# The opening of a two-block transformer kernel: c as a small tile, four modulation tiles on TensorE, another order of the first products

## What is computed

```python
c_act = silu(c)                              # c: 1 x 1024
mod = c_act @ ada_w[0] + ada_b[0]            # 6 x 1024; shift_t, scale_t are its first two parts
h = rmsnorm(x, norm_g[0, 0]) * (1.0 + scale_t) + shift_t
q, k, v, r, a_lr = split(h @ w_in)           # gated linear attention follows
```

## Time and profile before

| | us |
|---|---|
| three runs | 1540.8, 1542.72, 1542.75 |
| median | 1542.72 |
| the profiled execution | 1540.82 |
| its span | 1539.5 |
| TensorE, VectorE, ScalarE busy | 1513.5, 985.3, 660.6 |
| mean granted TensorE clock | 0.999 of 2.4 GHz |

### The profile page before, as it was taken

The page is one execution under the profiler, slowest core; times in us unless marked ns, Lnnn a source line. Parts: engine busy times, 40 slices in busy tenths (PEclk is TensorE's granted clock), DMA queues, the critical chain, the costliest instruction groups (busy, mean ns, idle before and its releaser), DMA issues.

```text
span 1539.5 us, 18851 instructions
## 1 busy us (share of the span) xinstructions
PE 1513.5 (98%) x7498; PEld 1235.9 (80%) x7498; DVE 985.3 (64%) x1592; ACT 660.6 (43%) x1118; POOL 163.9 (11%) x153
## 2 busy tenths in 40 slices
PE   8999999999999999999999999999999999999998
PEld 6778878888888888777777878888888876888776
DVE  7567667866666664777776743434344539989764
ACT  6445434513233233455565532413233436555660
POOL 0000002000000002111111100000000102675200
PEclk9999999999999999999999999999999999999999
DMA  9344444566656553122212243333333222212131
GB/s 370 120 129 148 140 137 161 167 215 192 194 189 200 185 162 98 55 69 69 69 56 83 96 117 96 96 96 96 98 94 102 72 87 68 70 53 75 37 109 55
DMA packets 52458, 181.82 MB, mean 118 GB/s; under 512 B 5793, under 2 KB 6689, under 8 KB 52370
## 3 DMA queue, kind: packets, MB, share of 16 engines
q1 hardware_dynamic: 52370, 180.61, 37.4%
HBM read 177.05 MB, written 3.41 MB: 117 GB/s over the span
## 4 chain that ended last, share of the span: by engine, by line
PE 90%; DVE 4%; ACT 2%; POOL 2%; DMA 1%; issue 1%; SPq 0%; DVEq 0%; ACTq 0%
PE PS L520 24%; PE PS L523 23%; PE PS L521 23%; PE PS L530 2%; PE PS L531 2%; PE PS L533 2%; PE PS L576 2%; PE PS L912 1%; PE PS L757 1%; PE PS L776 1%; PE PS L595 1%; PE PS L1067 1%; POOL sb_TMD L2345 1%; PE PS L1061 1%; PE PS L1062 1%; DMA sb_rg<-ada 1%
## 5 line engine op out<-in xcount | busy, mean ns | idle before, releaser
L520 PE MATMUL PS<-sb_Hh,sb_Wh 128*128 128x512 f32 (+1 forms) x1016 | 404.8, 398 | 2.8 <-DVE sb_Hl L1708 2.8
L523 PE MATMUL PS<-sb_Hh,sb_Wl 128*128 128x512 f32 (+1 forms) x1016 | 396.0, 390 | 0.6 <-DVE sb_Wl L1677 0.6
L521 PE MATMUL PS<-sb_Hl,sb_Wh 128*128 128x512 f32 (+1 forms) x1016 | 396.0, 390 | 0.0
L1111 ACT ACTIVATE sb_Wh<-sb_RAW 128x1024 fp32r<-128x1024 f32 (+1 forms) x218 | 228.3, 1048 | 289.9 <-PE PS L523 283.0
L1677 DVE TENSOR_TENSOR sb_Wl<-sb_RAW,sb_Wh 128x1024 fp32r<-128x1024 f32 (+1 forms) x218 | 268.1, 1230 | 83.7 <-ACT sb_Wh L1111 83.6
L520 PEld LDWEIGHTS PS<-sb_Hh,sb_Wh 128*128 128x128 f32 (+1 forms) x1016 | 189.6, 187 | 59.6 <-issue 16.0
L520 PE MATMUL PS<-sb_Oh,sb_Wh 128*128 128x512 f32 x600 | 235.2, 392 | 0.4 <-ACT sb_rg L1295 0.4
L523 PE MATMUL PS<-sb_Oh,sb_Wl 128*128 128x512 f32 x600 | 233.7, 389 | 0.0
L521 PE MATMUL PS<-sb_Ol,sb_Wh 128*128 128x512 f32 x600 | 233.5, 389 | 0.0
L523 PEld LDWEIGHTS PS<-sb_Hh,sb_Wl 128*128 128x128 f32 (+1 forms) x1016 | 189.6, 187 | 42.9 <-DVE sb_Wl L1677 1.1
L521 PEld LDWEIGHTS PS<-sb_Hl,sb_Wh 128*128 128x128 f32 (+1 forms) x1016 | 189.8, 187 | 39.9 <-issue 1.2
(11 more groups left out here) (376 smaller groups left out, 2041.1 us busy)
## 6 DMA issues: line engine op xcount, KB each, us to landing
sb_RAW<-w SPq DMA_DIRECT2D x128, 512.0 KB, 3.6
sb_ARW<-ada SPq DMA_DIRECT2D x86, 512.0 KB, 4.5
sb_RAW<-diff_in SPq DMA_DIRECT2D x24, 512.0 KB, 3.7
sb_RAW<-gla_in SPq DMA_DIRECT2D x20, 512.0 KB, 3.7
sb_RAW<-in_b SPq DMA_DIRECT2D x16, 512.0 KB, 3.8
sb_RAW<-gla_wo SPq DMA_DIRECT2D x8, 512.0 KB, 3.6
sb_RAW<-diff_wo SPq DMA_DIRECT2D x8, 512.0 KB, 3.6
sb_RAW<-wo SPq DMA_DIRECT2D x8, 512.0 KB, 3.7
```

The costliest lines, as they stand in the source:

```text
L520: mm(to[0:m, :], WH[si][:, k, 0:m], hi[:, k, :], start=first, stop=False)
L521: mm(to[0:m, :], WH[si][:, k, 0:m], lo[:, k, :], start=False, stop=False)
L523: ins = mm(to[0:m, :], WL[si][:, k, 0:m], hi[:, k, :], start=False, stop=last)
L1111: act(WH[slot_of(b)][:, :, 0:m], RAWS[raw_of(b)][:, 0:8 * m].rearrange("p (k m) -> p k m", k=8), ACT.Copy).then_inc(*done("w_hi", b))
```

## The change

- c arrives as `c8`, 128 x 8, and silu works on that tile. A product with an identity matrix (128 columns of `con`, put in `RS` for the time being) makes a block-diagonal matrix; ones x that matrix gives silu(c) in every partition, and VectorE copies it to `CB`.
- Modulation tiles 0 to 3 lie turned in memory. TensorE multiplies each (eight slices of 128 x 128) with the eight columns of silu(c); VectorE adds the bias. The other 92 stay as they were.
- The scale, and an f32 h in `SSQ`, of steps 0 and 1 come from VectorE.
- ScalarE makes the rstd before the first two weight blocks' high parts.
- In TensorE's loop blocks 0 and 1 take, at each step, both products with the high activation first and then the one with the low.
- Fillers, VectorE's order and the order of the transfers are changed accordingly: modulation tile 2j + 2 now stands ahead of `h_low_first(j)`, not 2j + 4.

```diff
@@ -271,6 +271,7 @@
         MOD = sb("MOD", [P, 2, 48])
         SC = sb("SC", [P, 4, 8])
         nbr = sb("nbr", [P, 8])
+        c8 = sb("c8", [P, 2, 8])
         epsb = sb("epsb", [P, 2])
         relb = sb("relb", [32, 4])
         rb = sb("rb", [32, 4, 128])
@@ -310,6 +311,8 @@
         WH = [Wh[:, n] for n in range(3)] + [OV(Oh, n) for n in range(4)] + [W3h[:], W5h[:]]
         WL = [Wl[:, n] for n in range(3)] + [OV(Ol, n) for n in range(4)] + [W3l[:], W5l[:]]
         CPS = PS[:, 0:2, :].rearrange("p a t -> p (a t)")
+
+        MV = lambda s: PS[:, 5 if s < 2 else 1, s % 2:s % 2 + 1]
         flat = lambda x: x.rearrange("p a t -> p (a t)")
         RAWS = [RAW[:, n, :] for n in range(3)] + [flat(x[:]) for x in (qd, ki, ksT, sct)]
         AW = [ARW[:, n, :] for n in range(3)] + [flat(x) for n in range(2) for x in (gvT[:, n], rg[:, n])]
@@ -426,7 +429,8 @@
                 skew = bass.AP(tensor=ap.tensor, offset=ap.offset + 127, ap=[[639, 128], [1, 512]])
                 e.op.dma_start(TBIAS[h], skew).then_inc(*landed(f"bias{h}", h))
 
-            e.op.dma_start(CB[0:1, :], D["c"]).then_inc(*landed("c"))
+            e.op.dma_start(c8[:, 0, :], D["c8"]).then_inc(*landed("c"))
+            e.op.dma_start(RS[:, 0:128], D["con"][:, CON["ident"][0]:CON["ident"][0] + 128]).then_inc(*landed("eye"))
             xT = D["xT"].rearrange("(c p) t -> p c t", p=P)
             for n in range(4):
                 e.op.dma_start(X[:, 2 * n:2 * n + 2, :], xT[:, 2 * n:2 * n + 2, :]).then_inc(*landed(f"x{n}", n))
@@ -438,7 +442,9 @@
                 if j == 0:
                     weights(1)
                     weights(0)
-                if j < 5:
+                elif j == 1:
+                    weights(2)
+                if 0 < j < 5:
                     weights(j + 2)
             e.op.dma_start(wa2[:], D["w_a2"]).then_inc(*landed("wa2"))
             e.op.dma_start(con[:], D["con"]).then_inc(*landed("con"))
@@ -599,20 +605,47 @@
                 for _ in range(n):
                     mm(PS[:, 6, 0:128], ones[:], ones[:], start=True, stop=True)
 
+            def mod_first(s):
+                e.wait_ge(at(f"ada{ada_buf(s)}", s), at("c_silu"))
+                for k in range(8):
+                    ins = mm(MV(s), AW[ada_buf(s)][:, k * 128:(k + 1) * 128], c8[:, 0, k:k + 1], start=k == 0, stop=k == 7)
+                ins.then_inc(*done("mv", s))
+
             e.wait_ge(at("one"))
             busy(8)
-            e.wait_ge(at("c"))
+            e.wait_ge(at("c_diag"))
             for n in range(2):
-                ins = mm(PS[:, n, :], ones[0:1, :], CB[0:1, n * T:(n + 1) * T], start=True, stop=True)
+                ins = mm(PS[:, n, :], ones[:], TMD[:, n, :], start=True, stop=True)
             ins.then_inc(*done("c_row"))
-            busy(8)
             for j in range(8):
                 e.wait_ge(at("sq", 0, j))
                 mm(PS[:, 7, :], ones[:], TA.buf(("sq", 0, j)), start=j == 0, stop=j == 7).then_inc(*done("stat", 0, j))
-            busy(16)
+            mod_first(0)
+            mod_first(1)
+            e.wait_ge(at("cact"))
+            mod_first(2)
+            busy(2)
+            def two_first(k):
+                e.wait_ge(at("h_hi", 0, k))
+                for b in range(2):
+                    m = block_size(b)
+                    if k == 0:
+                        open_block(b)
+                    mm(bank(b)[0:m, :], WH[b][:, k, 0:m], Hh[:, k, :], start=k == 0, stop=False)
+                    e.wait_ge(at("w_lo", b))
+                    mm(bank(b)[0:m, :], WL[b][:, k, 0:m], Hh[:, k, :], start=False, stop=False)
+                e.wait_ge(at("h_lo", 0, k))
+                for b in range(2):
+                    m = block_size(b)
+                    ins = mm(bank(b)[0:m, :], WH[b][:, k, 0:m], Hl[:, k, :], start=False, stop=k == 7)
+                    if k == 7:
+                        ins.then_inc(*done("proj", b))
+
             for j in range(8):
-                e.wait_ge(at("h_lo", 0, j))
-                for b in (0, 1, 2, 6, 3, 4, 5):
+                two_first(j)
+                if j == 0:
+                    mod_first(3)
+                for b in (2, 6, 3, 4, 5):
                     if b < j + 2 or b == 2 and j == 0:
                         if j == 0:
                             open_block(b)
@@ -621,7 +654,7 @@
                     open_block(j + 2)
                     for k in range(j + 1):
                         add_k(j + 2, k, (Hh, Hl), k == 0, False)
-                busy({0: 10, 1: 4}.get(j, 0))
+                busy({0: 4, 1: 4}.get(j, 0))
 
 
             def gla_gates(h):
@@ -1148,10 +1181,13 @@
                 A, Bc_, layer, which = AB[0]
                 src = TD.buf(("xn", 0, j))
                 e.wait_ge(at("mod", 0, j))
-                act(A[:, j:j + 1], MOD[:, 0, 8 + j:9 + j], ACT.Identity, scale=V("n00", j),
-                    bias=V("n00", j)).then_inc(*done("sca", j))
-                e.wait_ge(at("sca", j), at("xn", 0, j))
+                if j > 1:
+                    act(A[:, j:j + 1], MOD[:, 0, 8 + j:9 + j], ACT.Identity, scale=V("n00", j),
+                        bias=V("n00", j)).then_inc(*done("sca", j))
+                e.wait_ge(at("sca" if j > 1 else "sc_first", j), at("xn", 0, j))
                 act(Hh[:, j, :], src, ACT.Identity, scale=A[:, j:j + 1], bias=Bc_[:, j:j + 1]).then_inc(*done("h_hi", 0, j))
+                if j < 2:
+                    return
                 to, free = TA.take(("hf", 0, j), ("h_lo", 0, j))
                 e.wait_ge(*free)
                 act(to, src, ACT.Identity, scale=A[:, j:j + 1], bias=Bc_[:, j:j + 1]).then_inc(*done("h_f", 0, j))
@@ -1208,30 +1244,31 @@
 
 
             e.op.preload_act_table_set("natural_log_exp_and_others")
-            e.wait_ge(at("vec"))
-            cs = TMD[:].rearrange("p a t -> p (a t)")
+            cs = c8[:, 1, :]
             def square_first(j):
                 to, free = TA.take(("sq", 0, j), ("stat", 0, j))
                 e.wait_ge(at(f"x{j // 2}", j // 2), *free)
                 act(to, X[:, j, :], ACT.Square).then_inc(*done("sq", 0, j))
 
-            e.wait_ge(at("c_row"))
-            act(cs, CPS, ACT.Exp, scale=-1.0).then_inc(*done("c_exp"))
-            square_first(0)
-            square_first(1)
+            e.wait_ge(at("c"))
+            act(cs, c8[:, 0, :], ACT.Exp, scale=-1.0).then_inc(*done("c_exp"))
             e.wait_ge(at("c_one"))
             act(cs, cs, ACT.Ln).then_inc(*done("c_ln"))
             e.wait_ge(at("c_ln"))
             act(cs, cs, ACT.Exp, scale=-1.0).then_inc(*done("c_inv"))
-            for j in range(2, 8):
+            for j in range(8):
                 square_first(j)
+            e.wait_ge(at("c_diag"))
+            rstd(PS[:, 7, :], at("stat", 0, 7), RS[:], (0,))
             w_hi(1)
             w_hi(0)
-            rstd(PS[:, 7, :], at("stat", 0, 7), RS[:], (0,))
+            e.wait_ge(at("vec"))
             for j in range(8):
                 h_tile(j)
-                if j < 5:
-                    w_hi(j + 2)
+                if j == 0:
+                    w_hi(2)
+                if j < 4:
+                    w_hi(j + 3)
 
 
             def gates_first(h):
@@ -1699,13 +1736,16 @@
                     ada(ADA_AT[b])
 
             def x_norm_first(j):
-                to, free = TD.take(("xn", 0, j), ("h_f", 0, j))
+                to, free = TD.take(("xn", 0, j), *([("h_f", 0, j)] if j > 1 else [("h_first", j), ("h_hi", 0, j)]))
                 e.wait_ge(at("rstd", 0), *free)
                 tt(to, X[:, j, :], RS[:], ALU.mult).then_inc(*done("xn", 0, j))
 
             def h_low_first(j):
-                e.wait_ge(at("h_f", 0, j))
-                tt(Hl[:, j, :], TA.buf(("hf", 0, j)), Hh[:, j, :].bitcast(F), ALU.subtract).then_inc(*done("h_lo", 0, j))
+                if j < 2:
+                    e.wait_ge(at("h_first", j), at("h_hi", 0, j))
+                else:
+                    e.wait_ge(at("h_f", 0, j))
+                tt(Hl[:, j, :], TA.buf(("hf", 0, j)) if j > 1 else SSQ[:], Hh[:, j, :].bitcast(F), ALU.subtract).then_inc(*done("h_lo", 0, j))
 
             def x_norm(i, j, s):
                 x, r = X[:, j, HALF[s]], RS[:, HALF[s]]
@@ -1764,34 +1804,63 @@
                 ts(s, s, 1e18, 1.0, ALU.min, ALU.add).then_inc(*done("s_one", b))
 
 
-            cs = TMD[:].rearrange("p a t -> p (a t)")
+            def mod_first(s):
+                layer, t = ADA_TILES[s]
+                e.wait_ge(at("mv", s | 1), at("vec"))
+                ts(MOD[:, layer, t:t + 1], MV(s), V("ada_b", t), None, ALU.add).then_inc(*done("mod", layer, t))
+
+            def h_first(j):
+                A, Bc_, layer, which = AB[0]
+                e.wait_ge(at("mod", 0, j))
+                ts(A[:, j:j + 1], MOD[:, 0, 8 + j:9 + j], 1.0, V("n00", j), ALU.add, ALU.mult).then_inc(*done("sc_first", j))
+                e.wait_ge(at("sc_first", j), at("xn", 0, j))
+                if j:
```

(52 more changed lines are left out.)

## The result

| | before | after |
|---|---|---|
| median, us | 1542.60 (8 runs, 1540.80 to 1544.87) | 1546.76 (8 runs, 1543.37 to 1550.17) |
| ratio, 95% interval | | 1.0025 (1.0014 to 1.0037) |
| the profiled execution, its span | 1540.82, 1539.5 | 1546.67, 1545.4 |
| mean granted clock of TensorE | 0.999 | 0.995 |
| `wa2` product starts | 65.26 | 69.46 |

The changed kernel is 4.2 us slower, by the medians and by the start of `wa2`; that is 1.8 us more than the forecast's sum. Everything up to the product with `wa2` can be read in TensorE's timeline of the changed kernel (start, length, line, shapes; idle time before in brackets); it answers to the earlier trace rows.

What follows compares the result with a forecast made beforehand. TensorE bounds the kernel, but in the opening VectorE's queue releases j = 2: 2.55 late, minus 0.9 for high products ahead, plus 0.8 of waits, 2.4 us longer, giving 1545.1 us; range 1541.5 to 1549.5.

Steps and rivals of the forecast that it cites:

- the forecast's sum: Over the opening: low part of j = 2 late by 2.55, minus 0.9, plus 0.8, so 2.4 us longer.
- the forecast's own range: Kernel time expected for the favoured case, its mild variant included: 1543.1 to 1546.8 us.
- the forecast's case: In the opening, the new VectorE wait makes the kernel 2.4 us longer; chance 0.58 with the mild variant.
- Steps 1 and 2: Opening: c8 lands at 3.0, silu(c) is spread by products, and the statistics end at 14.5, 2.4 earlier.
- Step 3: TensorE's column products after the statistics: sixteen records, 1.8 us per modulation tile, two tiles done at 18.1.
- Step 4: First h tile: high part at 20.4, low weights at 21.7, five products to 22.9.
- The rival in which the start decides: Opening: the earlier first high product is what counts, winning 2.5 to 3.2 us; chance 0.07.
- Step 5: VectorE waits for tile 3, issued behind all of step j = 0, until 24.9; idle 2.6 us.
- Steps 6 and 7: VectorE and ScalarE behind the new wait: low part of j = 2 ends at 34.9, 2.55 late.
- Step 8: TensorE from j = 2: high products ahead gain 0.9, two waits at j = 3 cost 0.3 and 0.5, none later.
- The clock's fall: TensorE drops to its lower clock near 19 in one-column products, adding 3.4 to 5.2 us to 2.4; chance 0.22.
- The argument against a fall: Opening: an earlier TensorE gap of 2.30 at 22.90, with 128-column fillers ahead, had cost no clock.

Runs made afterwards that it cites:

- edit 4: Changed kernel with blocks 0 and 1 taking all their products behind the low part of h again; median 1546.08 us, ratio 1.0025.
- edit 8: Changed kernel run once more, unedited, for more runs and a second profile; median 1548.23 us, ratio 1.0039.
- edit 1: Changed kernel with 128 equal moving columns instead of one in the column products; median 1543.37 us, ratio 1.0010.
- edits 10 and 11: Former: changed kernel with 128 columns, early tile 3, VectorE reordered, high products not ahead, ratio 0.9997; latter: kernel before with small c alone, 1.0003.
- edit 2: Changed kernel with TensorE's fourth column product (tile 3) moved ahead of step j = 0, still one column; median 1543.59 us, ratio 1.0005.

## Why the prediction was right, and where it was not

The median, 1546.76, lies at the upper edge of the forecast's own range, and the change is slower by 0.25% where "within 0.2%" had the larger chance. That it lies inside that range is in part luck: it is the forecast's sum with, on top, a fall of the clock that the forecast's case left out.

Steps 1 and 2 (small c, c row). c8 was taken by ScalarE at 2.55, not 3.0, and the statistics ended at 14.0, not 14.5. By the Trainium skill, DMA: Bandwidth & Descriptors, in its part on the anatomy of one DMA, the estimate was 2.7; issued at 0.72, it was there 1.83 later, a little under the page's 2.0, and 1.6 later in others of these executions. The page's part is on transfers issued from GpSimd, and this one was issued by SyncE, so no run here tests that figure. The step named the landing of c8 and the price of the product as risks, but not that VectorE needs the identity as well, nor that the product may find the lower clock. In the profiled execution of after neither showed; in edit 4 they cost 2.5.

Step 3 (column products). Sixteen records in 1.8 us, 0.112 each, was exact as long as the clock was up. The bounds for dear loads and for cheap ones were not needed.

Step 4 (first h tile). High part at 18.21, low weights by 21.2, products from 21.23: within 0.8 of the forecast, and hidden by the wait, as said. The rival in which the start decides is refuted: the first product of the opening came 1.67 earlier than at the earlier trace rows and the kernel is slower.

Step 5 (the new wait) is what the change costs. The edits name it from both sides: 2.61 with the clock held, and L - C falls by 2.69 when tile 3 is put ahead of step 0.

Steps 6 and 7. From the wait's end to the low part of j = 2 the sum had 34.2 - 24.9 = 9.3; after has 35.70 - 26.11 = 9.59.

Step 8. The two waits of j = 3 are there: its high products start at 40.66, its low ones at 42.09, each behind a record that started at 40.12 and 41.37, so 0.31 and 0.49 later than a distance of 0.23 gives; forecast were 0.3 and 0.5. High products ahead are worth 0.73 by the trace, forecast 0.9. Behind j = 3 there is no wait. Of 69.46 - 67.7 = 1.8, the late release is 1.2 (26.11 for 24.9), steps 6 and 7 are 0.3 and what follows 0.3. The column products had started 0.66 earlier than forecast, and the clock took that as well.

So the sum of 2.4 is what the kernel loses with the clock held: edit 1 with its start moved back by 0.87 has `wa2` at 67.83, 2.6 behind before, and its median ratio is 1.0010, 1.5 us, with an interval (0.2 to 2.9 us) that holds the 2.4. **What failed is the choice among the rivals.** The clock's fall had 0.22 and the forecast's case 0.58; every one of the fourteen runs of the changed kernel (after and edit 8) has a mean clock of 0.994 to 0.997, every one of edit 1's eleven 0.998 or 0.999. The mean alone would not do as a sign, since 0.996 and 0.997 occur in edits 10 and 11 too and 0.998 once each in edits 2 and 4; the stretches of the traces name the place. The argument against a fall leaned on a gap behind 128-column fillers, and wrote beside it that those had 128 columns; that difference was the whole matter. The Trainium skill, TensorE: Matmul & The Clock Gate, Part 1, calls the lower level the default that activity lifts. The trace neither bears that out nor contradicts it, but it shows that a TensorE without idle time can go down: it did so in mid-stream, and edit 1 shows that the one column made the difference.

The size of that rival was high as well: 3.4 to 5.2 on top of 2.4, against 1.6 to 1.8 in the trace. It began at 17.7, before the 19 that was named, and tile 2 and step 0 ran at half speed, but tile 3 found the clock rising (2.14 for it, where edit 2's took 3.55), and the second fall, 28 to 31, was hidden by the wait before j = 2. The measured 4.2 lies between the forecast's 2.4 and the clock case's 5.8 to 7.6.

What stays open: the medians of after and of edit 8 lie 3.4 and 4.9 above edit 1's (2.3 and 4.5 by the ratios), more than the 1.6 and 0.4 that their openings explain. The variable start and the falls near 1260 differ from run to run and may be part of it; no run here separates them.

## What to carry to other kernels

Moving work from a late engine to an idle one pays only if the results come back in the order in which the late engine needs them; here one tile issued behind the wrong step cost 2.6, where the four instructions taken off VectorE brought 0.4 once it was moved and the clock held. A stream of weight loads with one moving column each kept TensorE busy and yet lost it the clock; widening the moving side cost nothing and held it. Ahead of a start that everything hangs on, ask for each operand when it lands and at which clock its product runs, since a cover in the old order may have hidden both.

## What the runs showed of the hardware

- One or 128 moving columns cost the same, 0.112 us a record, with a full-width weight load for each; at the lower level the one-column record took 0.21.
- A busy TensorE can fall to its lower level: the granted clock was 1.00 to about 17.7 and 0.50 from 18, with one-column records back to back since 13.84 (after); with 128 columns it was 1.00 over the column products in all six executions.
- At the start records ran at half speed though the profile's granted clock says 1.00, and for how long differs: four 512-column records that began between 4.8 and 5.9 took 3.78 us in three executions, 1.98 or 1.99 in four, 2.36 and 2.96 in two.
- The identity (64 KB), issued at 1.16, was first used 2.5 to 3.4 us later where VectorE waited for it; c8 (4 KB) 1.6 to 1.8 after its issue.
